# Constant multiplies in five waits of the tensor engine: a one-core transformer block with a mixture of experts

## The chip, the core and the metric

The kernel runs on one core of one Trainium2 chip. The metric is device time in microseconds (us) of one execution. Three runs of the kernel before took 2674.59, 2674.87 and 2675.00 us (median 2674.87). A core has a tensor engine (PE, matrix products; its weight loads are PEld), a vector engine (DVE), a scalar engine (ACT), GpSimd (POOL, which here issues gathers and scatters) and SyncE (SP, which issues the other transfers). Each engine works through its own instructions in order and waits on semaphores for the others.

## The reference, cut to what matters

1024 latent tokens of width 1024 pass through a token mixer (convolutions, a scan, a Hyena branch and gates), then through a mixture of experts. The change lies between the two. What is computed there:

```python
mix = merged @ w_out
h1 = layer_norm(alpha * x + gate * mix)
u = modulate(h1, shift, scale)
g_logits, e_logits = u @ rt_group_w + rt_group_b, u @ rt_expert_w + rt_expert_b   # 4 groups, 32 experts
g_sel = argmax(g_logits); top_v, top_i = top_k(e_logits[g_sel], 2)
weights = softmax(top_v) * softmax(g_logits)[g_sel]
# the 2048 (token, expert) pairs are sorted by expert into blocks of 128 rows
for block, e in blocks:
    y = (silu(xb @ w_gate[e]) * (xb @ w_up[e])) @ w_down[e]
out = layer_norm(alpha * h1 + gate2 * sum of y * weight)
```

## The kernel before, in words

The stage `stage_experts` holds four pieces that run one after the other on each engine. All code on the engines is written out in order by hand; nothing is scheduled. Line numbers are those of the kernel before.

1. **Projection and routing**, over 8 tiles `t` of 128 tokens. `project(t)` (lines 2591 to 2604) makes the output projection of one tile. `turn(t)` (2606 to 2613) transposes the tile `u` by eight transposes into banks 4 and 5 of PSUM, ACT copies it out as `u_chan` (2743), and `route(t)` (2615 to 2622) multiplies it in eight steps with the router's 36 columns into bank 6. The loop at 2624 runs `project(t)`, `route(t-2)`, `turn(t-1)`, so its last turns are `route(6)`, `turn(7)`, `route(7)`.
2. **The choice**. DVE alone finds the groups, the experts and the number of earlier pairs of each expert, in a chain of short operations (2871 to 2901). PE sums these counts over the tokens with three multiplies (2637 to 2640, "rank"). DVE works out each pair's place in the sorted list (2905 to 2941), PE turns that into lists of indices with sixteen multiplies (2643, "ids"), and DVE writes them as integers (2943 to 2948). ACT takes part at two points: two casts of expert weights and a table load stand ahead of the exponential (2753, 2758) for which DVE waits before line 2875.
3. **The first gather**. POOL gathers 128 token rows of block 0 (2556), PE transposes them (`turn_x`, 2652), ACT casts the result (`x_up`, 2776) and DVE writes what the cast lost (`x_lo`, 2973). Ahead of that operation DVE has two differences of weights, `rest_chunk(0, 0, 0)` and `(0, 0, 1)` (2822).
4. **The experts**, 32 fixed blocks and a number of extra ones that depends on the input. Each block multiplies its 128 rows with 6 MB of weights, in three passes (2664 to 2666: upper by upper, lower by upper, upper by lower parts of the numbers). The first 24 multiplies of a block are 512 columns wide and need `x_lo` (semaphore `x_ready`) and the first two chunks of weights (`whole`). Weights of blocks 0 and 1 are loaded early; those of later blocks when the parts in use come free (`used`).

PE waits at the head of `route(6)` (`u_chan_ready` and `logit_ready`), of the rank (`rank_in`), of the ids (`hot_ready`), of `turn_x(0)` (`x_in`) and of block 0 (`x_ready`).

A product of two plain 32-bit operands (f32) runs as two passes and leaves two records in the trace; one of operands in the rounded form (fp32r), and a transpose, leave one. An example of the first kind with both operands 128 by 128 stands in the scan, eight times in a kernel:

```python
                    for g in range(GROUPS):      # GROUPS = 4, line 1484
                        mm = nc.tensor.matmul(ps[:, 2, g * P:(g + 1) * P], b_chan[:, b, g, :], c_chan[:, b, g, :],
                                              start=True, stop=True)
```

`k.ones` is 128 by 128, f32, and all ones; `k.const("ident")` is 128 by 128, f32, the identity. With `k.ones` as the weights the program also makes the eight multiplies of line 2586, 512 columns wide.

Of the kernel before, what the change touches and what calls it, by code (L numbers as in the profile page):

```python
# [27 lines left out]
P = 128  # L28
# [3 lines left out]
TT = T // P  # L32
# [2358 lines left out]
def stage_experts(k, rows, weights, plan, merged, merged_rest, early_in):  # L2391

    nc, a, ps = k.nc, k.a, k.ps
# [5 lines left out]
    with k.stage("ex") as (sb, sem):  # L2399
# [103 lines left out]
        with nc.Block() as block:  # L2503
# [79 lines left out]
            def _(pe):  # L2583
                for part in range(LATE):
                    for h, (lo, hi) in enumerate(HALVES):
                        mm = nc.tensor.matmul(ps[:, 2 * part + h, :], k.ones[:, :], rows[:, part, lo:hi],
                                              start=True, stop=True)
# [3 lines left out]
                def project(t):  # L2591
                    if t >= 2:
                        pe.wait_ge(mix_read, t - 1)
                    pe.wait_ge(m_split, t + 1)
                    for kt in range(KT):
                        if t == 0:
                            pe.wait_ge(w_split, kt + 1)
                        up, lo_part = m_up[:, t % RING, kt, :], merged_rest[:, kt, t * P:(t + 1) * P]
                        for h, (lo, hi) in enumerate(HALVES):
                            bank = ps[:, 2 * (t % 2) + h, :]  # L2600
                            nc.tensor.matmul(bank, up, w_up[:, kt, lo:hi], start=(kt == 0), stop=False)
                            nc.tensor.matmul(bank, lo_part, w_up[:, kt, lo:hi], start=False, stop=False)
                            mm = nc.tensor.matmul(bank, up, w_lo[:, kt, lo:hi], start=False, stop=(kt == KT - 1))
                    mm.then_inc(mix_mm, 1)

                def turn(t):
                    pe.wait_ge(u_ready, t + 1)
                    if t:
                        pe.wait_ge(u_chan_ready, t)
                    for kt in range(KT):  # L2610
                        mm = nc.tensor.transpose(ps[:, 4 + kt // 4, (kt % 4) * P:(kt % 4 + 1) * P],
                                                 u[:, t, kt * P:(kt + 1) * P], k.const("ident"))
                    mm.then_inc(u_turned, 1)

                def route(t):
                    pe.wait_ge(u_chan_ready, t + 1)
                    if t:
                        pe.wait_ge(logit_ready, t)
                    for kt in range(KT):
                        mm = nc.tensor.matmul(ps[:, 6, 0:36], u_chan[:, kt, :], w_rt[:, kt, :],  # L2620
                                              start=(kt == 0), stop=(kt == KT - 1))
                    mm.then_inc(logit_mm, 1)

                for t in range(TT + 2):
                    if t == 1:
                        pe.wait_ge(rows_ready, 4)
                        pe.wait_ge(small_in, 64)
                    if t < TT:
                        project(t)
                    if t >= 2:  # L2630
                        route(t - 2)
                    if 1 <= t <= TT:
                        turn(t - 1)

                pe.wait_ge(rank_in, 1)
                rows_of = "p t e -> p (t e)"
                nc.tensor.matmul(ps[:, 0, 0:TT * E], k.ones[:, :], before.rearrange(rows_of), start=True, stop=False)
                nc.tensor.matmul(ps[:, 0, 0:TT * E], k.const("before"), chosen.rearrange(rows_of),
                                 start=False, stop=True)
                nc.tensor.matmul(ps[:, 1, 0:E], k.ones[:, :], every, start=True, stop=True).then_inc(rank_mm, 1)  # L2640
                pe.wait_ge(hot_ready, 2)
                for n in range(2 * TT):
                    mm = nc.tensor.matmul(ps[:, 7, 0:SLOTS], in_block[:, n, :], of_block[:, n, :],
                                          start=(n == 0), stop=(n == 2 * TT - 1))
# [5 lines left out]
                def turn_x(b):  # L2650
                    for kt in range(KT):
                        mm = nc.tensor.transpose(ps[:, 2 + kt // 4, (kt % 4) * P:(kt % 4 + 1) * P],
                                                 x[:, b, kt * P:(kt + 1) * P], k.const("ident"))
                    mm.then_inc(x_mm, 1)
# [8 lines left out]
                def three(out, left_up, left_lo, w_up, w_lo, first, last):  # L2663
                    nc.tensor.matmul(out, left_up, w_up, start=first, stop=False)  # L2664
                    nc.tensor.matmul(out, left_lo, w_up, start=False, stop=False)  # L2665
                    return nc.tensor.matmul(out, left_up, w_lo, start=False, stop=last)  # L2666

                pe.wait_ge(x_in[0], 16)
                turn_x(0)

                def body(i, b, j):
                    pe.wait_ge(x_ready, i + 1)
# [507 lines left out]
```

## Time and profile before

| quantity | value |
|---|---|
| median of three runs | 2674.87 us |
| the profiled execution's own time | 2678.04 us |
| its span | 2675.9 us |
| PE busy | 2448.5 us, 92% of the span |
| DVE busy | 1628.6 us, 61% |
| ACT busy | 937.7 us, 35% |
| mean granted TensorE clock | 0.953 of full |
| experts, first multiply to the last | about 1959 to 2603 us |

The granted clock is 1.00 (2.4 GHz) or 0.50 (1.2 GHz) at any time; a mean between the two is a mix. The profiled execution took 3.17 us more than the median of the runs, so a difference worked out from its rows is applied to 2674.87.

In a timeline row the first number is the start, the second the time from the first start to the last end of the instructions merged in it, and what stands in brackets is how long the engine was idle before and who released it. Starts of PE's records overlap: a record lasts longer than the distance to the next one, so the price of a multiply in a row of multiplies is the distance between starts. Its ends are modelled.

### The profile page before, as it was taken

The numbers are of one execution on the slowest core, as the hardware profiler recorded it, in microseconds if no ns is written. First come the engines' busy times: TensorE is split into PE (matmuls) and PEld (weight loads), VectorE is DVE, ScalarE is ACT, GpSimd is POOL, SyncE is SP. The second block draws the span as 40 slices with busy tenths as digits, with TensorE's granted clock in tenths as the row PEclk, the third lists the DMA queues.
The fourth block names the chain that finished last, engine by engine and source line by source line (L and its number), as shares of the span: only waits on it lengthen the run. The fifth ranks groups of instructions, "written<-read, shape, count | busy, mean of one in ns | idle before, by whom it ended". The sixth has DMA issues, their size and how long they took to land. (4 is left out here: it accounts for less than half of the span.)

```text
span 2675.9 us, 30511 instructions
## 1 busy us (share of the span) xinstructions
PE 2448.5 (92%) x11864; PEld 1978.1 (74%) x11864; DVE 1628.6 (61%) x1628; ACT 937.7 (35%) x1088; POOL 291.3 (11%) x250
## 2 busy tenths in 40 slices
PE   7879989989997879999999999999689999999984
PEld 3338878768886878787877787878578888888871
DVE  4453369833322764432786535657688898888876
ACT  3132321142321433101111100021247777777763
POOL 3310000000102320000000000100011221221210
PEclk9899989989998989999999999999789999999997
DMA  5341145312324323111111113543659999999946
GB/s 175 133 142 40 40 144 182 128 51 72 111 92 152 102 82 105 43 48 46 48 40 48 36 48 103 173 172 118 259 212 365 374 355 366 367 369 388 386 175 251
DMA packets 95119, 437.49 MB, mean 163 GB/s; under 512 B 16057, under 2 KB 28617, under 8 KB 80299
## 3 DMA queue, kind: packets, MB, share of 16 engines
q1 hardware_dynamic: 68330, 357.81, 36.5%
q0 software_dynamic: 26688, 78.30, 8.4%
q8 instruction: 69, 1.13, 0.2%
q14 instruction: 32, 0.25, 0.0%
HBM read 401.51 MB, written 55.51 MB: 171 GB/s over the span
## 5 line engine op out<-in xcount | busy, mean ns | idle before, releaser
L387 PE MATMUL ps<-uT_upper_rest,ring_rest 128*128 128x512 f32 x1296 | 515.8, 398 | 0.0
L387 PEld LDWEIGHTS ps<-uT_upper_rest,ring_rest 128*128 128x128 f32 x1296 | 246.7, 190 | 62.9
L2666 PE MATMUL ps<-ex_u_raw_rest,uT_rest 128*128 128x256 f32 x560 | 157.4, 281 | 0.0
L387 PE MATMUL ps<-uT_upper_rest,xbc_upper 128*128 128x512 f32 x336 | 136.6, 406 | 7.6 <-DVE ring_rest L816 7.6
L387 PE MATMUL ps<-uT_upper_rest,cs_upper 128*128 128x512 f32 x320 | 130.0, 406 | 11.2 <-DVE ring_rest L816 6.0
L2664 PE MATMUL ps<-ring_rest,uT_rest 128*128 128x256 f32 (+1 forms) x416 | 135.0, 325 | 3.1 <-DVE uT_rest L2973 2.4
L2664 PE MATMUL ps<-ex_upper,uT_rest 128*128 128x256 f32 (+1 forms) x424 | 135.0, 318 | 0.0
L387 PE MATMUL ps<-uT_rest,xbc_upper 128*128 128x512 f32 x336 | 134.9, 401 | 0.0
L2665 PE MATMUL ps<-ex_upper,uT_rest 128*128 128x256 f32 (+1 forms) x424 | 134.0, 316 | 0.0
L2665 PE MATMUL ps<-ring_rest,uT_rest 128*128 128x256 f32 (+1 forms) x416 | 133.0, 320 | 0.0
L387 PE MATMUL ps<-uT_rest,cs_upper 128*128 128x512 f32 x320 | 128.8, 402 | 0.0
L2563 POOL DMA_INDIRECT y_rows<-sb_uT,ex_scatter_at x35 | 92.4, 2641 | 298.7 <-ACT sb_uT L2772 289.5
L2666 PE MATMUL ps<-merged_rest,ex_hid_up 128*128 128x512 f32 x280 | 110.6, 395 | 0.0
L2666 PE MATMUL ps<-uT_upper_rest,uT_rest 128*128 128x512 f32 x280 | 110.4, 394 | 0.0
L2666 PEld LDWEIGHTS ps<-ex_u_raw_rest,uT_rest 128*128 128x128 f32 x560 | 105.3, 188 | 0.0
L2231 DVE SCALAR_TENSOR_TENSOR sb_y_aT<-cs_val,sb_cols,sb_y_aT 128x64 f32<-128x64 f32 (+14 forms) x120 | 90.2, 752 | 4.1
L387 PE MATMUL ps<-uT_upper_rest,hp_upper 128*128 128x512 f32 x192 | 78.0, 406 | 13.7 <-DVE ring_rest L816 13.7
L2664 PEld LDWEIGHTS ps<-ring_rest,uT_rest 128*128 128x128 f32 x416 | 78.8, 189 | 14.0 <-DVE uT_upper_rest L2822 5.3
L2822 DVE TENSOR_TENSOR uT_upper_rest<-sb_spare,ring_rest 128x2048 fp32r<-128x2048 f32 x36 | 80.9, 2289 | 10.0 <-ACT ring_rest L2749 10.0
L2664 PEld LDWEIGHTS ps<-ex_upper,uT_rest 128*128 128x128 f32 x424 | 79.6, 188 | 9.2 <-DVE uT_upper_rest L2822 3.1
L2665 PEld LDWEIGHTS ps<-ex_upper,uT_rest 128*128 128x128 f32 x424 | 79.9, 188 | 6.1
L2822 DVE TENSOR_TENSOR merged_rest<-sb_merged,ring_rest 128x2048 fp32r<-128x2048 f32 x36 | 82.3, 2287 | 2.3 <-ACT ring_rest L2749 2.3
(494 smaller groups left out, 6081.0 us busy)
## 6 DMA issues: line engine op xcount, KB each, us to landing
sb_spare<-in_ex_g SPq DMA_DIRECT2D x35, 2048.0 KB
ex_u_raw<-in_ex_u SPq DMA_DIRECT2D x35, 2048.0 KB, 10.4
sb_merged<-in_ex_d SPq DMA_DIRECT2D x35, 2048.0 KB
ring<-in_conv SPq DMA_DIRECT2D x32, 512.0 KB, 3.4
ring<-in_w_gate SPq DMA_DIRECT2D x32, 512.0 KB, 3.3
md_piece<-in_w_late POOLq DMA_DIRECT2D x32, 512.0 KB, 5.4
ring<-in_w_ssd SPq DMA_DIRECT2D x21, 512.0 KB, 3.4
ring<-in_w_mod SPq DMA_DIRECT2D x16, 512.0 KB, 3.4
```

The costliest lines, as they stand in the source:

```text
L387: last = self.nc.tensor.matmul(out, weight, x[:, k, lo:hi], start=(k == 0 and n == 0), stop=(k == kt - 1 and n == 2))
L2231: ins = nc.vector.scalar_tensor_tensor(out=acc[:, lo:hi], in0=val[:, t, lo + s * GRID_W:hi + s * GRID_W], scalar=weight, in1=acc[:, lo:hi] ...
L2563: pool.indirect_dma_start(out=a["y_rows"], out_offset=bass.IndirectOffsetOnAxis(scatter_at[:, i:i + 1], 0), in_=y, in_offset=None, bounds_ ...
L2664: nc.tensor.matmul(out, left_up, w_up, start=first, stop=False)
L2665: nc.tensor.matmul(out, left_lo, w_up, start=False, stop=False)
L2666: return nc.tensor.matmul(out, left_up, w_lo, start=False, stop=last)
L2822: nc.vector.tensor_tensor(chunk(rest, m, b), chunk(raw, m, b), slot(m, b).bitcast(F32), ALU.subtract).then_inc(whole, 1)
```

## The change

A helper `keep_busy(bank, n)` issues `n` multiplies of `k.ones` with the identity into one bank of PSUM. It is called at five places, ahead of five waits: 44 before `route(6)`, 72 before the rank, 84 before the ids, 36 before `turn_x(0)` and 14 before block 0, 250 in all. Nothing reads what they write, no semaphore is raised by them, and banks 4 and 7 hold no live data there. Each stands behind the work ahead of it and in front of the wait; PE works in order, so what stands behind a wait also stands behind the added multiplies.

```diff
+                def keep_busy(bank, n):
+                    for _ in range(n):
+                        nc.tensor.matmul(ps[:, bank, 0:P], k.ones[:, :], k.const("ident"), start=True, stop=True)
+
...
                     if t < TT:
                         project(t)
+                    if t == TT:
+                        keep_busy(7, 44)
                     if t >= 2:
                         route(t - 2)
...
+                keep_busy(4, 72)
                 pe.wait_ge(rank_in, 1)
...
                 nc.tensor.matmul(ps[:, 1, 0:E], k.ones[:, :], every, start=True, stop=True).then_inc(rank_mm, 1)
+                keep_busy(4, 84)
                 pe.wait_ge(hot_ready, 2)
...
+                keep_busy(4, 36)
                 pe.wait_ge(x_in[0], 16)
                 turn_x(0)
+                keep_busy(4, 14)
```

PE's instructions from the last projection to block 0, before. L2620 is `route`, L2611 `turn`, L2637 to L2640 the rank, L2643 the ids, L2652 `turn_x`, L2664 the first multiply of block 0:

```order
L2620 MATMUL ps<-ex_w_rt,ex_su 128x36 x8
L2611 MATMUL ps<-sb_consts,sb_uT 128x128 x8
L2620 MATMUL ps<-ex_w_rt,ex_su 128x36 x8
L2611 MATMUL ps<-sb_consts,sb_uT 128x128 x8
L2620 MATMUL ps<-ex_w_rt,ex_su 128x36 x8
L2637 MATMUL ps<-sb_y_aT,sb_ones 128x256
L2638 MATMUL ps<-sb_y_aT,sb_consts 128x256
L2640 MATMUL ps<-sb_y_aT,sb_ones 128x32
L2643 MATMUL ps<-ex_of_block,ex_in_block 128x48 x16
L2652 MATMUL ps<-sb_consts,sb_uT 128x128 x8
L2664 MATMUL ps<-ring_rest,uT_rest 128x512
```

The order of the same engine after, from the first `route` of the last iterations to the rank; L2617 is the new multiply, L2624 is `route`:

```order
L2624 MATMUL ps<-ex_w_rt,ex_su 128x36 x8
L2611 MATMUL ps<-sb_consts,sb_uT 128x128 x8
L2617 MATMUL ps<-sb_consts,sb_ones 128x128 x44
L2624 MATMUL ps<-ex_w_rt,ex_su 128x36 x8
L2611 MATMUL ps<-sb_consts,sb_uT 128x128 x8
L2624 MATMUL ps<-ex_w_rt,ex_su 128x36 x8
L2617 MATMUL ps<-sb_consts,sb_ones 128x128 x72
L2645 MATMUL ps<-sb_y_aT,sb_consts 128x256
```

And from the rank on to block 0 after the change, where L2660 is `turn_x` and L2672 the first multiply of block 0:

```order
L2644 MATMUL ps<-sb_y_aT,sb_ones 128x256
L2645 MATMUL ps<-sb_y_aT,sb_consts 128x256
L2647 MATMUL ps<-sb_y_aT,sb_ones 128x32
L2617 MATMUL ps<-sb_consts,sb_ones 128x128 x84
L2651 MATMUL ps<-ex_of_block,ex_in_block 128x48 x16
L2617 MATMUL ps<-sb_consts,sb_ones 128x128 x36
L2660 MATMUL ps<-sb_consts,sb_uT 128x128 x8
L2617 MATMUL ps<-sb_consts,sb_ones 128x128 x14
L2672 MATMUL ps<-ring_rest,uT_rest 128x512
```

Nothing changes place among the older instructions; 250 multiplies are put between them on PE, and the other engines keep theirs.

## Rows read from the trace of the kernel before

**Rows 1.** Windows of ten us: busy of each engine, PEclk, DMA share, GB/s

```profile
1890.00:1900.00 10.00, 10.00 (x49) 8.20 (x47) 5.59 (x7) 0.20 (x1) 1.07 (x2) 1.00 0.26 105
...
1920.00:1930.00 10.00, 0.00 (x0) 0.00 (x0) 8.49 (x35) 0.62 (x2) 0.00 (x0) 0.50 1.01 431
...
1980.00:1990.00 10.00, 10.00 (x68) 9.12 (x67) 9.95 (x6) 6.84 (x5) 2.69 (x1) 1.00 0.97 357
1990.00:2000.00 10.00, 10.00 (x51) 8.20 (x50) 7.95 (x8) 8.81 (x8) 1.02 (x1) 1.00 0.89 329
```

**Rows 2.** Timeline of PE, from the last projections to block 0

```profile
1899.30 1.87 PE L2620 MATMUL ps<-ex_w_rt,ex_su 128*128 128x36 f32 x16
1901.00 1.07 PE L2611 MATMUL ps<-sb_consts,sb_uT 128*128 128x128 f32 x8
1909.10 3.60 PE L2620 MATMUL ps<-ex_w_rt,ex_su 128*128 128x36 f32 x16 [7.03 <-DVE ex_logits L2827]
1912.50 1.95 PE L2611 MATMUL ps<-sb_consts,sb_uT 128*128 128x128 f32 x8
1915.55 3.63 PE L2620 MATMUL ps<-ex_w_rt,ex_su 128*128 128x36 f32 x16 [1.10 <-ACT ex_su L2743]
1930.43 1.22 PE L2637 MATMUL ps<-sb_y_aT,sb_ones 128*128 128x256 f32 x2 [11.25 <-DVE sb_y_aT L2901]
...
1932.30 0.47 PE L2640 MATMUL ps<-sb_y_aT,sb_ones 128*128 128x32 f32 x2
1945.44 3.61 PE L2643 MATMUL ps<-ex_of_block,ex_in_block 128*128 128x48 f32 x16 [12.67 <-DVE ex_in_block L2941]
1954.57 1.97 PE L2652 MATMUL ps<-sb_consts,sb_uT 128*128 128x128 f32 x8 [5.51 <-DMA sb_uT<-u_tok,ex_gather_at]
1958.90 0.79 PE L2664 MATMUL ps<-ring_rest,uT_rest 128*128 128x512 f32 x1 [2.36 <-DVE uT_rest L2973]
...
1962.64 0.40 PE L2664 MATMUL ps<-ring_rest,uT_rest 128*128 128x512 f32 x1
...
1966.08 0.28 PE L2664 MATMUL ps<-ex_upper,uT_rest 128*128 128x256 f32 x1
```

**Rows 3.** One line each: records, ns of one (min, median, max), first and last start

```profile
L2620 PE MATMUL ps<-ex_w_rt,ex_su x128: 193/279/426, 1830.5 to 1918.8; 128*128 128x36 f32 x128
L1484 PE MATMUL ps<-scan_c_chan,scan_b_chan x64: 273/275/328, 884.9 to 976.3; 128*128 128x128 f32 x64
L2586 PE MATMUL ps<-sb_y_aT,sb_ones x16: 592/592/1193, 1786.5 to 1795.6; 128*128 128x512 f32 x16
```

**Rows 4.** Timeline of PE in the scan

```profile
884.92 1.05 PE L1484 MATMUL ps<-scan_c_chan,scan_b_chan 128*128 128x128 f32 x8
```

**Rows 5.** Timeline of ACT around the choice

```profile
1914.49 1.01 ACT L2743 COPY ex_su<-ps 128x1024 f32<-128x1024 f32 x1 [10.51 <-PE ps L2611]
1915.40 3.70 ACT L2753 CAST ring_rest<-sb_spare 128x2048 fp32r<-128x2048 f32 x2
1919.11 1.28 ACT L2758 ACT_TABLE_LOAD   x1
```

**Rows 6.** Timeline of DVE around the choice

```profile
1920.67 0.19 DVE L2875 TENSOR_REDUCE sb_y_aT<-sb_y_aT 128x8 f32<-128x32 f32 x1 [0.58 <-ACT sb_y_aT L2758]
...
1932.81 0.19 DVE L2905 COPY sb_y_aT<-ps 128x32 f32<-128x32 f32 x1 [2.35 <-PE ps L2640]
...
1949.09 0.21 DVE L2943 TENSOR_SCALAR ex_none<-ps 128x48 f32<-128x48 f32 x1 [3.70 <-PE ps L2643]
...
1953.02 4.49 DVE L2822 TENSOR_TENSOR uT_upper_rest<-sb_spare,ring_rest 128x2048 fp32r<-128x2048 f32 x2
1957.62 1.23 DVE L2973 TENSOR_TENSOR uT_rest<-ps,uT_rest 128x1024 fp32r<-128x1024 f32 x1
```

**Rows 7.** Windows in which the granted clock stayed or changed, columns as above

```profile
880.30:883.70 3.40, 2.86 (x13) 2.89 (x14) 0.63 (x1) 1.63 (x7) 0.00 (x0) 0.50 0.27 72
...
1911.00:1917.50 6.50, 5.40 (x26) 5.00 (x26) 0.20 (x1) 3.01 (x3) 0.00 (x0) 0.50 0.99 418
```

## The prediction

> **What bounds the kernel now.** I read the busy shares by windows first. In the windows before 1900 us and again from 1970 us on, PE is busy all of the time at the full clock; between lie some 60 us in which it mostly waits, and the clock stands at 0.50, 1.2 GHz [rows 1]. So PE bounds the projection and the experts, and the choice of experts is a chain across engines. The experts hold no slack: 10.00 of 10 us in every window [rows 1], so a later or earlier start of block 0 moves the end by as much. Transfers have 0.89 to 0.97 of their share there, but later loads are released by PE's own progress and move with it.
>
> Then the timeline of PE in the gap [rows 2]. It shows five waits: 7.03 us before `route(6)`, 11.25 before the rank, 12.67 before the ids, 5.51 before `turn_x(0)` and 2.36 before block 0. It also shows what the low clock costs: `route` takes 1.87 us at 1899.30 and 3.60 at 1909.10; `turn` 1.07 against 1.95. Last the timelines of ACT and DVE, for what else would be late if PE were quicker.
>
> **The price of an added multiply.** It is f32, 128 by 128, and not a transpose. Line 1484 has this very shape. Its 8 x 4 = 32 multiplies left 64 records, `route`'s 64 left 128 [rows 3]: two records each. Eight records at the full clock span 1.05 us, of which the last is 0.275, so starts lie (1.05 - 0.275) / 7 = 0.111 us apart [rows 3, 4]. The records of `route` at 1899.30, with 36 columns, give (1.87 - 0.279) / 15 = 0.106 [rows 2, 3]; that one is pulled down by its first step. An added multiply costs 2 x 0.111 = 0.223 us (the unrounded spacing is 0.1115). From both sides: 2 x 0.106 = 0.212 by `route`, and 2 x 0.114 = 0.228 by the transposes at 1901.00, (1.07 - 0.27) / 7. I take 0.223, the row of the same shape and type. At half the clock it is 0.427: `route`'s sixteen records at 1909.10 give (3.60 - 0.40) / 15 = 0.213 each.
>
> So the added multiplies take 44 x 0.223 = 9.8 us, 16.1, 18.7, 8.0 and 3.1, against waits of 7.03, 11.25, 12.67, 5.51 and 2.36. Each group is longer than its wait. PE works in order, and the work behind waits for the last of them. That is the heart of the forecast.
>
> **The chain, step by step.** The last slot of `turn(6)` ends near 1901.9 [rows 2].
>
> - 44 multiplies end at 1911.7. `route(6)` could have begun at 1909.10 and is 2.6 late, but it and `turn(7)` now run at the full clock: 1.78 + 1.07 = 2.85 us where they took 1914.45 - 1909.10 = 5.35. They end at 1914.55, 0.1 later than before. ACT's copy begins with them [rows 5].
> - `route(7)` then ends 1.7 us earlier. That gains nothing: DVE needs the exponential before line 2875, and on ACT there stand the copy, two casts and a table load in a row, 1914.49 to 1920.4 [rows 5, 6]. DVE waited 0.58 us for it already. The choice runs 0.1 late.
> - 72 multiplies follow from 1917.4 and end at 1933.5, where the rank could begin at 1930.5. The rank's four wide records took 1930.43 to 1932.30, 1.87 us, so some 0.93 at the full clock; with two narrow ones the rank takes 1.1 us of PE's time. From here on PE never waits: 84 multiplies from 1934.6 to 1953.3, the ids 1.8 us (3.6 before), 36 to 1963.1, `turn_x` 0.9, 14 to 1967.1. The other engines are ready sooner each time. DVE reads the rank at 1934.8, 2.0 later than before, and has `hot_ready` at 1947.4 against 1953.3. It reads the ids at 1955.4 against 1949.09 [rows 6], 6.3 later, so the gathered rows land at 1960.9, before 1963.1. `x_lo` is done at 1966.6, before 1967.1.
> - Block 0 begins at 1967.1, and began at 1958.90: +8.2 us. Its 24 wide multiplies took 1966.08 - 1958.90 = 7.18, the first nine at half speed. At the full clock fifteen of them took 1966.08 - 1962.64 = 3.44, so 24 take 5.5: -1.7. DVE's next differences end at 1971.1, before they are needed. Net **+6.5 us**.
>
> The quicker `turn_x` would not pay even in time: DVE is at its two differences from 1953.02 to 1957.51, and takes `x_lo` at 1957.62 [rows 6].
>
> **Does the clock stay up?** From 1911.7 to 1917.4 stand `route(6)`, `turn(7)`, an idle 1.1 us and `route(7)`: narrow work. Before, the same work kept PE busy 5.40 of 6.50 us and the clock stayed at 0.50 [rows 7]. So I expect it to fall for a moment around 1915 to 1919 and the next dense group to bring it back. A short low stretch with PE dense in it is that of 880.30 to 883.70 [rows 7]; 3.4 us at half speed cost 1.7 us. From 1917.4 on PE is the bound, so it is paid in full. If it doesn't fall, 0; if it falls earlier or twice, 3.4. I take **+1.7**. The multiplies of ones at line 2586 run from 1193 to 592 ns within one dense row [rows 3], so dense work of this kind does raise the clock.
>
> The Trainium skill, "TensorE: Matmul & The Clock Gate", Part 4 on the transpose mode, says that transposes don't count as busy for the full clock. By it the fall is certain and the sum +8.2; without it +6.5 stays possible. The row can't tell transposes from narrow multiplies.
>
> The sum: 6.5 + 1.7 = +8.2 us. The profile's span would go from 2675.9 to 2684.1; against the median of the runs, 2674.87 + 8.2 = **2683.1 us**.
>
> **Rivals.**
>
> - *The multiplies fit their waits* (faster). It decides at the price of one: +8.2 changes by 250 us per us of it, so no change is reached near 0.19, and all five fit from about 0.15 down. Then PE is never late at full clock: `route(6)` and `turn(7)` -2.5 (ACT starts earlier as well), the rank 2.38 to 1.3, -1.1, the ids 3.65 to 2.0, -1.65, `turn_x` nothing behind DVE's differences, block 0 -1.7: -7.0, 2667.9. For it speaks only that the waits at half clock are plain in the trace. Against it are 64 records for 32 multiplies at 0.111 [rows 3, 4].
> - The Trainium skill, "TensorE: Matmul & The Clock Gate", section "Back-to-back issue gap", gives about 81 ns per matmul of 128 columns in a stream of loads and multiplies. By it an added multiply of two passes would be an estimated 0.162 and the sum about -6, near 2669. This trace has 111 ns, and the trace decides.
> - *No difference*: part of the delay is taken up behind block 0, or the price is 0.20. It needs +5.3 or less of the 8.2. For it: transfers are close to their full share, so the experts might not follow PE alone. Against: PE is never idle there. It would give 2675 to 2680.
> - *The clock stays at 0.50 in spite of the added work* (the change doesn't do what it says). Then 250 x 0.427 = 106.8 and the work between, 16.8, follow 1901.9: block 0 at 2025.5, +66.6, about 2741. Against it is line 2586.
>
> **How the numbers follow.** About 0.2% (5.3 us) is what a measurement of this kernel can tell from no change. The forecast with one short fall of the clock has 0.60; without a fall (2681.4) 0.15; with a longer one (2685 to 2687) 0.10; the clock low throughout 0.02. These are slower: 0.87. No difference 0.07, faster 0.06. The bounds of the price, 0.212 and 0.228, move the sum by 250 x -0.011 = -2.7 and 250 x 0.005 = +1.3. Range: 2678.5 (no fall, lower price: 2681.4 - 2.7) to 2686.5 (a second low stretch, 3.4 in all, and the dearer price).
>
> **What would show it.** The added multiplies in pairs of records 0.111 apart, 500 in all. `route(6)` near 1911.7. DVE's line 2875 still waiting for ACT, at about 1920.8. No idle of PE ahead of the rank, the ids, `turn_x` and block 0, where 11.25, 12.67, 5.51 and 2.36 us stood. Block 0 at 1967 to 1969, its first 24 multiplies in 5.5 us. A low clock for a few us near 1918 and no other until the end of the experts. I am wrong if an added multiply costs clearly less than 0.2 us, if PE idles behind the groups, or if the experts' stretch gets shorter.

## The result, and the profile after

The kernel after takes 2679.99 us (median of 13 runs) against 2674.71 us before (13 runs). The ratio is 1.0022 with a 95% interval of 1.0014 to 1.0029, so 5.9 us slower, between 3.7 and 7.8; the two medians by themselves differ by 5.28. The profiled execution took 2679.96 us with a span of 2677.4 us. The forecast was +8.2, or 2683.1 us. One execution of e10_fit_again took 5046.05 us, where its other six took 2662 to 2669; it counts as slow and is left out of the ratio.

The two profiles differ in two places that have to be kept apart. From the start of `turn(6)` to the first 256-column multiply of block 0 (its 25th) the profile before has 1966.08 - 1901.00 = 65.08 us [rows 2], the one after 1968.38 - 1895.01 = 73.37: **+8.29**. But `turn(6)` begins 5.99 us earlier in the profile after, in code that the change doesn't touch. This second difference is the subject of e1_none and e9_after_again. "Local" below always means the stretch between those two points, against 65.08.

The timeline of PE after, with the same columns as [rows 2]; L2617 is the added multiply, L2624 `route`, L2644 to L2647 the rank, L2651 the ids, L2660 `turn_x`, L2672 block 0:

```profile
1895.01 1.07 PE L2611 MATMUL ps<-sb_consts,sb_uT 128*128 128x128 f32 x8
1895.91 9.99 PE L2617 MATMUL ps<-sb_consts,sb_ones 128*128 128x128 f32 x88
1905.74 1.87 PE L2624 MATMUL ps<-ex_w_rt,ex_su 128*128 128x36 f32 x16
1907.45 1.07 PE L2611 MATMUL ps<-sb_consts,sb_uT 128*128 128x128 f32 x8
1909.62 1.98 PE L2624 MATMUL ps<-ex_w_rt,ex_su 128*128 128x36 f32 x16 [1.10 <-ACT ex_su L2753]
1911.43 17.95 PE L2617 MATMUL ps<-sb_consts,sb_ones 128*128 128x128 f32 x144
1929.21 0.60 PE L2644 MATMUL ps<-sb_y_aT,sb_ones 128*128 128x256 f32 x2
...
1930.22 19.00 PE L2617 MATMUL ps<-sb_consts,sb_ones 128*128 128x128 f32 x168
1948.98 1.94 PE L2651 MATMUL ps<-ex_of_block,ex_in_block 128*128 128x48 f32 x16
1950.77 8.29 PE L2617 MATMUL ps<-sb_consts,sb_ones 128*128 128x128 f32 x72
1958.89 1.04 PE L2660 MATMUL ps<-sb_consts,sb_uT 128*128 128x128 f32 x8
1959.76 3.29 PE L2617 MATMUL ps<-sb_consts,sb_ones 128*128 128x128 f32 x28
...
1962.81 0.48 PE L2672 MATMUL ps<-ring_rest,uT_rest 128*128 128x512 f32 x1
...
1968.38 0.28 PE L2672 MATMUL ps<-ex_upper,uT_rest 128*128 128x256 f32 x1
```

All five waits of PE are gone; the one idle time in brackets is the pause of 1.10 us ahead of `route(7)`, which was there before. PE had waited for the other engines, and now they wait for PE. Between the two points everything runs at the full clock but for one stretch of 3.4 us from 1912.0 on, seen in the windows (columns as in [rows 1]):

```profile
1905.00:1911.00 6.00, 4.90 (x46) 4.66 (x44) 0.20 (x1) 2.45 (x2) 0.00 (x0) 1.00 1.03 436
1912.00:1915.40 3.40, 3.40 (x19) 3.40 (x18) 1.01 (x6) 2.67 (x3) 0.00 (x0) 0.51 1.00 424
1915.40:1930.00 14.60, 14.60 (x129) 14.52 (x129) 8.24 (x33) 5.19 (x4) 0.00 (x0) 1.00 0.98 410
```

The timeline of DVE after shows who waits instead, to be read against [rows 6]:

```profile
1914.74 0.19 DVE L2885 TENSOR_REDUCE sb_y_aT<-sb_y_aT 128x8 f32<-128x32 f32 x1 [2.24 <-ACT sb_y_aT L2768]
1930.42 0.19 DVE L2915 COPY sb_y_aT<-ps 128x32 f32<-128x32 f32 x1 [5.89 <-PE ps L2647]
1950.96 0.21 DVE L2953 TENSOR_SCALAR ex_none<-ps 128x48 f32<-128x48 f32 x1 [7.97 <-PE ps L2651]
1954.90 4.49 DVE L2832 TENSOR_TENSOR uT_upper_rest<-sb_spare,ring_rest 128x2048 fp32r<-128x2048 f32 x2
1961.01 1.23 DVE L2983 TENSOR_TENSOR uT_rest<-ps,uT_rest 128x1024 fp32r<-128x1024 f32 x1 [1.61 <-ACT uT_rest L2786]
```

DVE waits 5.89 us for the rank where it waited 2.35, and 7.97 for the ids where it waited 3.70. Its wait for ACT's exponential, ahead of line 2885, grew from 0.58 to 2.24: that is the 1.7 us that a quicker `route(7)` brought and nobody could use.

### The profile page after: what moved, and what is told of

It reads as the page before. It is cut to its first block and busy times, and to the rows that moved or that the text cites. A ratio compares the mean times of both kernels' runs of the same rounds, so it can differ in the third digit from the quotient of the medians.

```text
span 2677.4 us, 31511 instructions
## 1 busy us (share of the span) xinstructions
PE 2490.0 (93%) x12364; PEld 2022.8 (76%) x12364; DVE 1625.9 (61%) x1628; ACT 937.1 (35%) x1088; POOL 294.7 (11%) x250
## 5 line engine op out<-in xcount | busy, mean ns | idle before, releaser
L2672 PE MATMUL ps<-ex_upper,uT_rest 128*128 128x256 f32 (+1 forms) x424 | 134.9, 318 | 0.0
L2672 PE MATMUL ps<-ring_rest,uT_rest 128*128 128x256 f32 (+1 forms) x416 | 134.1, 322 | 0.7 <-DVE uT_upper_rest L2832 0.7
L2672 PEld LDWEIGHTS ps<-ring_rest,uT_rest 128*128 128x128 f32 x416 | 78.4, 188 | 11.0 <-DVE uT_upper_rest L2832 5.2
L2672 PEld LDWEIGHTS ps<-ex_upper,uT_rest 128*128 128x128 f32 x424 | 79.6, 188 | 9.2 <-DVE uT_upper_rest L2832 3.1
```

## The experiments

All are the kernel after with other counts, or with other columns. "Timed" is the ratio to the kernel before, less 1, times the median of the kernel before that was timed along with it, and its 95% interval.

| run | counts of added multiplies | local, us | local against 65.08 | timed, us |
|---|---|---|---|---|
| e1_none | none | 65.09 | 0.0 | +0.8 (-1.6 to +3.2) |
| after | 44, 72, 84, 36, 14 | 73.37 | +8.3 | +5.9 (+3.7 to +7.8) |
| e9_after_again | the same | 73.37 | +8.3 | +6.7 (+4.3 to +8.8) |
| e2_fit | 31, 4 in the pause, 56, 55, 24, 14 | 58.06 | -7.0 | -5.3 (-8.0 to -2.9) |
| e10_fit_again | the same | 58.04 | -7.0 | -9.1 (-12.3 to -5.9) |
| e3_half | 22, 36, 42, 18, 7 | 60.33 | -4.8 | -3.7 (-5.9 to -1.3) |
| e4_pause | as after, and 4 in the pause | 71.73 | +6.7 | +10.7 (+7.5 to +13.9) |
| e5_only_first | 44, then none | 65.14 | +0.1 | -2.9 (-5.1 to -0.5) |
| e6_without_first | 0, 72, 84, 36, 14 | 75.65 | +10.6 | +9.1 (+5.9 to +12.3) |
| e7_more_third | 44, 72, 124, 36, 14 | 82.27 | +17.2 | +16.6 (+13.1 to +20.1) |
| e8_only_third | 0, 0, 55, 0, 0 | 64.53 | -0.6 | -0.3 (-2.7 to +1.9) |
| e11_narrow | as after, 36 columns | 126.41 | +61.3 | +61.2 (+57.8 to +64.7) |

**e1_none**, all five calls taken out.

```diff
-                    if t == TT:
-                        keep_busy(7, 44)
...
-                keep_busy(4, 72)
...
-                keep_busy(4, 84)
...
-                keep_busy(4, 36)
...
-                keep_busy(4, 14)
```

> No added multiply at all, the instructions of the kernel before. Every theory expects a ratio of 1.000. What is asked is how far the stretch ahead of the choice differs between two profiles of the same instructions: turn(6) began at 1901.0 us in the profile before and at 1895.0 in the one after. If that is scatter between executions or chips, turn(6) begins anywhere from 1893 to 1902 here. If the added code itself makes the earlier part quicker (the rival), it begins near 1901 here and near 1895 in each kernel that has added multiplies.

The local stretch is the same within 0.01 us, but `turn(6)` begins at 1897.92 where the profile before has 1901.00. So identical instructions differ by 3 us ahead of it:

```profile
1897.92 1.07 PE L2611 MATMUL ps<-sb_consts,sb_uT 128*128 128x128 f32 x8
...
1963.01 0.28 PE L2668 MATMUL ps<-ex_upper,uT_rest 128*128 128x256 f32 x1
```

In the eleven profiles with added multiplies `turn(6)` begins between 1892.9 and 1900.5, which overlaps these two. Their mean is 1896.7, that of the two without is 1899.5. So it isn't shown that the added code makes the earlier part quicker, and with two profiles against eleven a small effect is not excluded.

**e2_fit**, counts from 0.223 us each, so that each group ends about when its wait does. The last group, 14 multiplies, is unchanged.

```diff
-                        keep_busy(7, 44)
+                        keep_busy(7, 31)
+                    if t == TT + 1:
+                        keep_busy(7, 4)
...
-                keep_busy(4, 72)
+                keep_busy(4, 56)
...
-                keep_busy(4, 84)
+                keep_busy(4, 55)
...
-                keep_busy(4, 36)
+                keep_busy(4, 24)
```

> Counts 31, 4 (in the pause between turn(7) and route(7)), 56, 55, 24 and 14, worked out from 0.223 us for one, so that each group ends just before what it waits for. Theory (the delay is only the overlength, and the full clock pays about 7 us on the chain): 6 to 7.5 us faster than the kernel before, no low clock between 1895 and 2600 us. Rival (DVE, ACT and the gather set the chain, the clock is worth little): 0 to 2 us faster.

Local -7.0, timed -5.3 (expected 6 to 7.5 faster, which lies inside the interval), and the clock is at 1.00 through the gap. Ahead of the rank and the ids short waits are back with their old releasers; ahead of `turn_x(0)` and block 0 the groups end with no idle time behind them (timeline of PE, then windows):

```profile
1904.96 1.95 PE L2624 MATMUL ps<-ex_w_rt,ex_su 128*128 128x36 f32 x16
...
1908.91 1.98 PE L2624 MATMUL ps<-ex_w_rt,ex_su 128*128 128x36 f32 x16 [0.21 <-ACT ex_su L2755]
...
1923.79 0.70 PE L2646 MATMUL ps<-sb_y_aT,sb_ones 128*128 128x256 f32 x2 [0.32 <-DVE sb_y_aT L2913]
...
1937.72 1.97 PE L2653 MATMUL ps<-ex_of_block,ex_in_block 128*128 128x48 f32 x16 [0.30 <-DVE ex_in_block L2953]
```

```profile
1890.00:1950.00 60.00, 59.05 (x488) 56.76 (x488) 41.48 (x110) 13.54 (x12) 4.67 (x5) 1.00 0.65 264
```

So with waits filled and not overrun, the full clock is worth the 7 us that the prediction gave to its first rival. That rival failed on the price of a multiply alone. This version is quicker than both kernels.

**e10_fit_again**, the same kernel.

> The kernel of counts 31, 4, 56, 55, 24, 14 once more, for its interval: -7.0 us between turn(6) and the 25th multiply of block 0 as in its first profile, and -5 to -8 in the timed runs. With the rival of an early part that gets quicker by 2 to 3 us, -9 to -10.

Local -7.0 again; timed -9.1. That value is outside the -5 to -8 that was expected and inside the -9 to -10 of the rival, by which the early part gets quicker; `turn(6)` begins at 1892.89, the earliest of all. The interval, -12.3 to -5.9, holds both, so this run decides nothing between them. The two measurements of this one kernel lie 3.8 us apart, and their intervals overlap.

**e3_half**, half of each count.

```diff
-                        keep_busy(7, 44)
+                        keep_busy(7, 22)
...
-                keep_busy(4, 72)
+                keep_busy(4, 36)
...
-                keep_busy(4, 84)
+                keep_busy(4, 42)
...
-                keep_busy(4, 36)
+                keep_busy(4, 18)
...
-                keep_busy(4, 14)
+                keep_busy(4, 7)
```

> Counts 22, 36, 42, 18 and 7, half of each. All groups end before their waits, with 2 to 5 us idle behind the larger ones. Theory: never late, but the clock falls in the idle rests, so that part of the real work is at 1.2 GHz: 3.5 to 6.5 us faster than the kernel before. Rival (any filling of two thirds of a wait keeps the clock up): 6.5 to 7.5 faster, no low clock in the gap.

Local -4.8. The clock fell twice: in `turn(7)` at 1909.7, behind an idle rest of 2.11 us and `route(6)`, and at 1940.4, inside the rest of 3.21 us ahead of the ids. It was low for 10.2 and 6.8 us, and `route(7)` and the ids ran at 1.2 GHz (timeline of PE, then windows):

```profile
1912.18 3.63 PE L2624 MATMUL ps<-ex_w_rt,ex_su 128*128 128x36 f32 x16 [1.10 <-ACT ex_su L2753]
...
1941.01 3.61 PE L2651 MATMUL ps<-ex_of_block,ex_in_block 128*128 128x48 f32 x16 [3.21 <-DVE ex_in_block L2951]
```

```profile
1909.70:1919.80 10.10, 9.00 (x42) 8.60 (x41) 3.11 (x20) 6.12 (x5) 0.00 (x0) 0.50 1.02 431
1920.00:1940.30 20.30, 16.67 (x144) 16.18 (x142) 17.30 (x58) 5.19 (x4) 0.00 (x0) 1.00 0.72 300
1940.40:1947.20 6.80, 6.19 (x29) 6.20 (x30) 2.92 (x9) 0.00 (x0) 0.33 (x1) 0.50 0.00 0
```

**e4_pause**, four more in the pause of 1.10 us.

```diff
+                    if t == TT + 1:
+                        keep_busy(7, 4)
```

> The kernel after, with 4 more multiplies in the pause of 1.1 us between turn(7) and route(7). Theory (the fall of the clock for 3.4 us comes from the narrow work and the pause together, and its 1.7 us are paid in full): no low clock, 1.7 us less than the kernel after, some 3.5 us over the kernel before. Rival (the pause doesn't matter, routing is too narrow by itself): the clock falls as before and the time is that of the kernel after, 5 to 6 over.

No low clock, and the group of 72 takes 16.32 us where it took 17.95. Local +6.7 where the kernel after has +8.3, so the fall cost 1.64 us. The four multiplies both shorten the pause to 0.21 us and put wider work between narrow, and this run doesn't tell which of the two kept the clock up. Windows, then timeline:

```profile
1900.00:1930.00 30.00, 29.79 (x263) 29.50 (x263) 13.75 (x50) 11.31 (x9) 1.07 (x2) 1.00 1.00 416
```

```profile
1911.55 16.32 PE L2617 MATMUL ps<-sb_consts,sb_ones 128*128 128x128 f32 x144
```

The timed runs say the opposite: +10.7, 4.8 us over the kernel after, where both the expectation and its rival had it at that kernel's time or below. The interval of this run, 7.5 to 13.9, doesn't hold its local value, and the profiled execution (2679.17 us) is the second lowest of the six. That the fall costs 1.64 us is shown between the two points of the trace alone; the timed difference is not explained.

**e5_only_first**, the first group alone.

```diff
-                keep_busy(4, 72)
...
-                keep_busy(4, 84)
...
-                keep_busy(4, 36)
...
-                keep_busy(4, 14)
```

> The first group of 44 alone. Theory: route(6) starts 2.6 us late and route(6) with turn(7) take 2.5 less, DVE's wait for ACT before the exponential hides what route(7) gains: 0.0 to +0.3 us. Rival (the late start is a plain loss): +2.6. Rival (the full clock in routing is a plain gain): -1.7.

Local +0.06: `route(6)` is late by 2.64 us, it and `turn(7)` are quicker by 2.57, and what `route(7)` gains is hidden behind ACT. The timed -2.9 (-5.1 to -0.5) is not explained by anything in the local stretch.

**e6_without_first**, the kernel after without its first group.

```diff
-                    if t == TT:
-                        keep_busy(7, 44)
```

> The kernel after without its first group. Theory: the first group is worth nothing, the rest is bound by the tensor engine from route(7) on. route(7) is now at 1.2 GHz (1.8 us longer), the group of 72 starts then at 1919.0 and its first 3.4 us or so are at the low clock, as in the kernel after: +1.5 to +1.8 us over the kernel after. Rival (the first group costs its 2.6 us): 2 us under the kernel after.

Local +10.6, 2.3 over the kernel after, more than the 1.5 to 1.8 expected. The group of 72 begins 1.56 us later after `turn(6)` (1914.80 - 1896.82 against 1911.43 - 1895.01), and takes 0.73 longer (18.68 against 17.95): 4.9 us of it lie at the low clock, against 3.4. The expectation had put in the same 3.4 (timeline of PE, then windows):

```profile
1896.82 1.07 PE L2611 MATMUL ps<-sb_consts,sb_uT 128*128 128x128 f32 x8
...
1914.80 18.68 PE L2617 MATMUL ps<-sb_consts,sb_ones 128*128 128x128 f32 x144
```

```profile
1914.80:1919.70 4.90, 4.90 (x24) 4.90 (x25) 3.67 (x21) 1.62 (x3) 0.00 (x0) 0.50 1.01 426
```

**e7_more_third**, 124 for 84 in the third group.

```diff
-                keep_busy(4, 84)
+                keep_busy(4, 124)
```

> The kernel after with 124 for 84 in the third group. Theory (the tensor engine is the bound from the second group to block 0, so every added multiply costs its 0.223 us): 40 x 0.223 = 8.9 us over the kernel after. Rival (part of a delay is taken up by the experts or their transfers): 5 to 7 us over.

Local 8.90 over the kernel after, timed 16.6 against 5.9 and 6.7. 248 records in 27.94 us are (27.94 - 0.275) / 247 = 0.112 each. The experts take up nothing of it: from the 25th multiply to the end of the span stand 2688.0 - 1978.38 = 709.6 us, where the kernel after has 2677.4 - 1968.38 = 709.0.

**e8_only_third**, 55 in the third group and no other.

```diff
-                        keep_busy(7, 44)
...
-                keep_busy(4, 72)
...
-                keep_busy(4, 84)
+                keep_busy(4, 55)
...
-                keep_busy(4, 36)
...
-                keep_busy(4, 14)
```

> The third group alone, 55 multiplies, which at 0.223 us and one low stretch of 3.4 us end 14.0 us after the rank where the ids are wanted after 12.7: late by 1.3 or, if the clock rises at once, not at all. Theory: ids quicker by 1.65, turn_x hidden, block 0 as before, so -1.7 to 0 us. Rival (the clock stays up for the whole rest once raised): -3 us or more.

The ids ran at the full clock, 1.94 us, but began 0.6 late. The clock was low again from 1945.9 to 1959.5, so it didn't stay up once raised. Local -0.6, within what was expected, and below what the timed runs can show.

**e9_after_again**, the kernel after unchanged.

> The kernel after once more. Its profile has 8.3 us more than that of before between turn(6) and the 25th multiply of block 0, its timed runs 5.9 us more with 3.7 to 7.8. Theory (the local 8.3 are the effect, and the stretch before turn(6) scatters by some us from one execution to the next): 8.3 us again between the same two points, and timed runs of +6 to +9. Rival (added code makes the early part 2 to 3 us quicker): timed +5 to +6 again and turn(6) near 1895.

Local 73.37 us, the same to the hundredth, with `turn(6)` at 1900.53 instead of 1895.01. Timed +6.7, inside the +6 to +9 that was expected. The rival of a quicker early part wanted `turn(6)` near 1895 and fails here. The two executions of this one kernel are already 3.5 us apart where line 1484 begins, at 884.3 and 887.8 us.

```profile
1900.53 1.07 PE L2611 MATMUL ps<-sb_consts,sb_uT 128*128 128x128 f32 x8
...
1973.90 0.28 PE L2672 MATMUL ps<-ex_upper,uT_rest 128*128 128x256 f32 x1
```

**e11_narrow**, 36 columns in each added multiply.

```diff
-                        nc.tensor.matmul(ps[:, bank, 0:P], k.ones[:, :], k.const("ident"), start=True, stop=True)
+                        nc.tensor.matmul(ps[:, bank, 0:36], k.ones[:, :], k.const("ident")[:, 0:36], start=True, stop=True)
```

> The kernel after with 36 columns for 128 in each of the 250 added multiplies. A record of 36 columns takes the same 0.111 us at the full clock and 0.213 at the low one, as route's do, so the price of one stays 0.223 or 0.427. Theory (narrow multiplies don't hold the clock, which is why it stayed at 0.50 in the routing and fell for 3.4 us in the kernel after): the clock falls in the first group and stays low to block 0, block 0 begins some 60 us later, +63 us in all. Rival (any busy tensor engine holds the clock): the time of the kernel after.

Local +61.3, timed +61.2, near the expected +63. The first group begins at the full clock; after 5.7 us in which PE did nothing but multiplies of 36 columns it falls, at 1901.2, and stays at 0.50 to 2017.2. PE is busy 113.90 of 115.00 us of that time (windows, then two groups of the timeline):

```profile
1895.40:1901.10 5.70, 5.70 (x54) 5.70 (x53) 5.50 (x9) 1.22 (x2) 0.53 (x1) 1.00 0.99 421
1902.00:2017.00 115.00, 113.90 (x523) 112.46 (x523) 35.43 (x99) 12.32 (x10) 2.62 (x3) 0.50 0.25 104
```

```profile
1895.40 13.57 PE L2617 MATMUL ps<-sb_consts,sb_ones 128*128 128x36 f32 x88
...
1918.67 30.91 PE L2617 MATMUL ps<-sb_consts,sb_ones 128*128 128x36 f32 x144
```

144 records in 30.91 us lie 0.213 apart. Between the two points PE idles only in the pause of 1.10 us, here as in the kernel after. What differs is the width of the added multiplies, and with it the clock: 0.50 for 116 us here, 0.50 for 3.4 us there.

## Why the prediction was right, and where it was off

- *The price of an added multiply, 0.223 us.* Right: 88 records in 9.99 us, (9.99 - 0.275) / 87 = 0.1117 each; the same from 248 records in e7_more_third. The nearest row, one of the same shape and type, was the one to take. The sum printed in the prediction, (1.05 - 0.275) / 7, gives 0.1107 and not the 0.1115 that it goes on with; by 0.1107 the forecast would have been 0.4 us lower.
- The 81 ns of the Trainium skill, "TensorE: Matmul & The Clock Gate", section "Back-to-back issue gap", don't hold for this kind of multiply, whose records lie 111.7 ns apart.
- *Each group is longer than its wait, and PE bounds the chain from the second group on.* Right: no idle time of PE from 1911.43 to the 25th multiply of block 0, and e7_more_third turned 40 multiplies into 8.90 us.
- *The first group is worth +0.1.* Right: +0.06 in e5_only_first. ACT's casts and table load hide what `route(7)` gains; DVE's wait there went to 2.24.
- *Routing, rank, ids and block 0 at the full clock.* Right. `route(6)` and `turn(7)` together take 1908.52 - 1905.74 = 2.78 against a forecast of 2.85. Block 0 needs 5.57 us for its first 24 multiplies against 5.5. With counts that fit, the whole local gain is 7.0 us, as forecast for the first rival.
- *The clock falls once, +1.7.* Right: one stretch of 3.4 us at 1912.0. e4_pause takes it away and gains 1.64. What was open in the prediction, transposes or narrowness, is half settled: in e11_narrow the clock fell behind 5.7 us of nothing but narrow multiplies. What transposes do to it was not tried.
- *The sum, +8.2.* Locally +8.29, twice. The timed +5.9 and +6.7 are lower, and the first interval ends at 7.8. The weak step is the last one: adding a local difference to the median, as if all else stood still. The part ahead of `turn(6)` scatters by some us between executions with the same instructions (1897.9 and 1901.0 without additions, 1895.0 and 1900.5 in the kernel after). Over the eleven measurements with added multiplies the timed difference is on average 0.4 us under the local one, by the table, with single ones from -3.0 to +4.0. So no lasting saving elsewhere is shown. But three of the eleven intervals, those of the kernel after, e4_pause and e5_only_first, don't hold their local value, so the timed runs vary by more than these intervals say.
- *Why the kernel after is timed 1.6 to 2.4 under its local value* stays open. A part shows in the profiles: from the 25th multiply to the end of the span stand 709.0 us in the kernel after and 708.7 in e9_after_again, 0.8 to 1.1 less than the 709.8 of the profile before and of e1_none. Most of it lies behind the experts, where one stretch of low clock runs from 2604.0 to 2627.9 before and from 2608.4 to 2628.8 after. It doesn't belong to the additions, for e4_pause and e7_more_third have 709.7 and 709.6.
- *The total.* 2679.99 us lies inside the stated range (whose ends, by the terms named there, come out at 2678.7 and 2686.0), but below 2683.1 and even below the 2681.4 given for no fall of the clock; the low end of the range stood for no fall and a lower price, and neither came true. So it owes that place in part to the width of the range and to the scatter. By the prediction's own bound of 5.3 us for no difference, the timed 3.7 to 7.8 doesn't exclude that rival. What excludes it is local: +8.29 twice, and nothing of 8.90 us taken up in e7_more_third.

## What to carry to other kernels

Fill a wait of the tensor engine only up to its length, with the price of a multiply taken from a row of the same shape and type: here the same idea gave +8.3 us with 250 multiplies and -7.0 with 184. Take multiplies of 128 columns, as here, and not of 36; fill the small pauses between narrow work as well, and look on the other engines for what will be late next. When an effect is as small as the scatter of the rest, measure it between two points of the trace that enclose it, and use the timed runs as a check.

## What the runs showed of the hardware

- A busy tensor engine is not enough for the full clock: 250 multiplies of 36 columns left it at 1.2 GHz for 116 us of almost unbroken work (e11_narrow). With the same weights, 250 of 128 columns held it at 2.4 GHz but for 3.4 us (the kernel after), and for all of the time with four more in the pause (e4_pause).
- At the full clock f32 records of 36 columns lie as far apart as those of 128, 0.111 to 0.112 us (`route` from its third record on, line 1484, the added ones), and at 1.2 GHz both 0.213. The two records of 256 columns of the rank take 1929.65 - 1929.21 = 0.44, so 0.22 each, twice as much. That a product is two records is shown; whether each is one pass through the array is not.
- The local stretch repeats to 0.02 us between two executions of the same instructions, while the part ahead of it differs by up to 7.6 us (start of `turn(6)` at 1892.89 to 1900.53 in kernels with additions, 5.5 of it in one and the same kernel).
